# Expert gate and up weights read in 4 KB pieces, gathered rows turned by every fourth column

## The reference, cut to what matters

```python
he = jax.nn.silu(t @ w_exp_gate[e]) * (t @ w_exp_up[e])      # t: tokens x 1024, weights 1024 x 256
out = out + dense_w[:, e:e+1] * (he @ w_exp_down[e])         # 256 x 1024; dense_w: two experts of 16 per token
```

## Time and profile before

| what | value |
|---|---|
| median of 3 runs | 900.63 us |
| span of the profiled execution | 897.8 us |
| TensorE busy / weight loads busy | 97% / 82% of the span |
| VectorE, ScalarE, GpSimd busy | 51%, 44%, 20% |
| DMA q1 (SP) / q0 (GpSimd) | 38.1% / 10.6% of 16 engines' span |
| packets of q1 / q0 | 89,240 / 7,904 |
| mean granted TensorE clock | 0.990 |

### The profile page before, as it was taken

One profiled execution on the slowest core, in us unless ns is written; L12 is line 12 of the kernel. 1 busy time (PEld: TensorE's weight loads), 2 busy tenths in 40 slices (PEclk: granted clock), 3 DMA queues, 4 the chain that ended last, 5 costly groups with the idle time before them and its releaser, 6 DMA issues.

```text
span 897.8 us, 13732 instructions
## 1 busy us (share of the span) xinstructions
PE 867.1 (97%) x5236; PEld 735.5 (82%) x5236; DVE 461.4 (51%) x762; ACT 393.2 (44%) x549; POOL 178.5 (20%) x129
## 2 busy tenths in 40 slices
PE   8999999999999999999999999999988999899996
PEld 7988888898788888888888878888887878688863
DVE  5411355455429642324231246613588887777737
ACT  5432444454432543333434112214444767587643
POOL 0001010000100001100100000400003586867651
PEclk9999999999999999999999999999989999999998
DMA  9324132332121313231220211792859999988787
GB/s 296 115 68 88 48 77 58 67 69 56 38 70 41 94 48 64 74 87 47 32 77 18 93 47 52 242 398 100 296 201 329 339 379 381 382 315 291 255 288 301
DMA packets 97227, 141.95 MB, mean 158 GB/s; under 512 B 4566, under 2 KB 75430, under 8 KB 97094
## 3 DMA queue, kind: packets, MB, share of 16 engines
q1 hardware_dynamic: 89240, 114.52, 38.1%
q0 software_dynamic: 7904, 26.44, 10.6%
q10 hardware_dynamic: 32, 0.26, 0.3%
HBM read 116.31 MB, written 24.90 MB: 157 GB/s over the span
## 4 chain that ended last, share of the span: by engine, by line
PE 84%; DVE 6%; DMA 4%; issue 2%; ACT 2%; POOL 1%; ACTq 0%; SPq 0%; POOLq 0%; DVEq 0%
PE main L850 22%; PE main L851 21%; PE main L852 21%; PE work L934 3%; PE work L904 2%; DMA xg<-h_rows,column 2%; PE work L1134 2%; PE work L967 2%; PE work L951 2%; PE work L921 1%; PE work L1081 1%; DMA x_in<-in_x_prompt 1%; PE work L850 1%; PE work L852 1%; PE work L851 1%
## 5 line engine op out<-in xcount | busy, mean ns | idle before, releaser
L850 PE MATMUL main<-ht_hi,w_hi 128*128 128x512 f32 (+1 forms) x576 | 198.5, 345 | 0.0
L851 PE MATMUL main<-ht_lo,w_hi 128*128 128x512 f32 (+1 forms) x576 | 194.0, 337 | 0.0
L852 PE MATMUL main<-ht_hi,w_lo 128*128 128x512 f32 (+1 forms) x576 | 193.9, 337 | 0.0
L1586 DVE TENSOR_TENSOR w_lo<-raw,w_hi 128x2048 fp32r<-128x2048 f32 x29 | 66.4, 2291 | 234.7 <-ACT w_hi L1264 234.7
L850 PEld LDWEIGHTS main<-ht_hi,w_hi 128*128 128x128 f32 x576 | 109.2, 190 | 18.7 <-issue 5.2
L852 PEld LDWEIGHTS main<-ht_hi,w_lo 128*128 128x128 f32 x576 | 109.2, 190 | 11.9
L851 PEld LDWEIGHTS main<-ht_lo,w_hi 128*128 128x128 f32 x576 | 109.4, 190 | 11.0
L850 PE MATMUL main<-w_hi,ht_hi 128*128 128x256 f32 (+1 forms) x304 | 95.6, 315 | 0.1
L702 POOL DMA_DIRECT2D bias<-bias_vectors x16 | 12.4, 774 | 408.4 <-DVE nmx L1652 176.4
L852 PE MATMUL main<-w_hi,ht_lo 128*128 128x256 f32 (+1 forms) x304 | 92.8, 305 | 0.0
L851 PE MATMUL main<-w_lo,ht_hi 128*128 128x256 f32 (+1 forms) x304 | 92.8, 305 | 0.0
(11 more groups left out here) (308 smaller groups left out, 1576.2 us busy)
## 6 DMA issues: line engine op xcount, KB each, us to landing
e_raw<-in_w_exp_gate SPq DMA_DIRECT2D x16, 1024.0 KB, 8.6
e_raw<-in_w_exp_up SPq DMA_DIRECT2D x16, 1024.0 KB, 10.5
e_raw<-in_w_exp_down SPq DMA_DIRECT2D x16, 1024.0 KB, 8.8
raw<-in_w_in SPq DMA_DIRECT2D x30, 512.0 KB, 5.2
expert_rows<-y_sb SPq DMA_DIRECT2D x18, 512.0 KB, 8.6
raw<-in_w_in SPq DMA_DIRECT2D x8, 1024.0 KB, 5.3
expert_rows<-y_sb SPq DMA_DIRECT2D x1, 5632.0 KB, 22.9
raw<-in_w_out SPq DMA_DIRECT2D x4, 1024.0 KB, 5.4
```

What stands on the lines that cost most here:

```text
L850: pe.matmul(out, s_hi, m_hi, start=(first and i == 0), stop=False)
L851: pe.matmul(out, s_hi, m_lo, start=False, stop=False)
L852: last = pe.matmul(out, s_lo, m_hi, start=False, stop=(final and i == n - 1))
L1586: dve.tensor_tensor(w_lo[:, c % 2, :], raw[:, c % 2, :], w_hi[:, c % 2, :], ALU.subtract).then_inc(s_wlo, 1)
```

## The change

The rows of a gate or up weight are dealt out in another way: row 512h + 4p + b goes to partition p, half h, block b. A partition then reads two pieces of 4 rows, 4 KB each, where it read 8 pieces of 1 KB. In `e_raw` the 2048 numbers of a partition are still 8 blocks of 256, block k = 4h + b, so the splits and the products are unchanged. Block k now sums over rows 512h + 4p + b, so the transposes must bring column 512h + 4p + b of the gathered rows to partition p: the weight load of each transpose takes every fourth column of a half (a step of 16 bytes) instead of 128 neighbouring columns. The rows in `h2_rows` and the gathers stay as they are.

```diff
-        gate_v = w_exp_gate[0].rearrange("e (k p) n -> e p k n", p=P)
-        up_v = w_exp_up[0].rearrange("e (k p) n -> e p k n", p=P)
+        gate_v = w_exp_gate[0].rearrange("e (h p b) n -> e p h (b n)", h=2, p=P)
+        up_v = w_exp_up[0].rearrange("e (h p b) n -> e p h (b n)", h=2, p=P)
...
-                put = e8 if c < 2 else e2
+                put = e2
                 sp.dma_start(put(e_raw[j % 2][:, c, :]), expert_v[c][e]).then_inc(s_eraw[c][j % 2], 16)
...
-                    last = pe.transpose(xt_ps[:, P * k:P * k + P], xg[:, j % 2, P * k:P * k + P], ident[:, :])
+                    last = pe.transpose(xt_ps[:, P * k:P * k + P], xg[:, j % 2, 512 * (k // 4) + k % 4:512 * (k // 4 + 1):4], ident[:, :])
```

## The result

The changed kernel takes 898.58 us against 900.67 (medians of 22 runs each); the ratio is 0.9972, with an interval of 0.9961 to 0.9982. It is faster by 0.3%, 2 to 2.5 us, where 7.0 us were forecast. Its runs go from 895.5 to 902.8 us, those of the kernel before from 898.3 to 903.7, and a profile shows one of them. Its profiled execution spans 896.7 us (897.8 before). SP's queue has 64,664 packets, 24,576 fewer, as worked out.

The account below looks back on a forecast made before the run. TensorE, busy 97% of the span, was taken as the bound, idling in the experts' first part for weights short of DMA. Transposes 0 less 7.0 us for pieces took 900.6 to 893.6 us, range 892 to 909.

Parts of the forecast that it names:

- Pieces, the bandwidth: Gate and up loads: 4 KB pieces raise 372 GB/s to at most 418, a tile's DMA taking 10.0 us; gain 7.0 us.
- No load is late: Experts' first 9 tiles: a shortage of 0.7 us per tile uses up 6 us of a lead of 10.
- Next late is nothing: with the waits gone TensorE's own 9.31 us bounds each tile: Experts' tiles: once the waits for late weights go, no other limit follows and TensorE's work sets the tile time.
- ScalarE's 3.06 us: GpSimd's split of the down weight started 3.06 us late behind ScalarE, which had waited for that weight; hence the late gather.
- every named wait: TensorE's waits of 0.83, 1.21 and 2.97 us, plus 1.8 of slow clock: 6.8 us by name, all expected to go.
- Transposes at 0: Strided weight loads of 152 transposes: cost taken as 0, with an upper bound of 12.0 to 19.3 us.
- About 48 ns to spare: Transposes' weight loads of 144 ns: loads of 192 ns still fit the pace of 0.109 us, so that growth is hidden.
- Rival 2: Part of the strided loads shows, 20 to 45 ns per transpose: 896.6 to 900.4 us, middle 898.5; chance 0.12.
- Rival 1: Strided weight loads set the transposes' pace, a column costing as much as in L1108: slower, middle 908.4 us; chance 0.26.
- The Trainium skill's rule on 16-byte lines: Full speed wants at least two hits per 16-byte memory line; the strided transposes hit a new line per column, giving rival 1.
- The third rival: No bandwidth gained where it is short, or gathers land later among 4 KB pieces: no change, 900.6 us; chance 0.10.
- The sum: Whole kernel: transposes 0 less 7.0 us for the pieces, so the median goes from 900.6 to 893.6 us.

Follow-up runs that it names:

- e7_early: Changed kernel, but GpSimd copies the table's column for the next gather ahead of its split of the down weight; 895.0 us, ratio 0.9933.
- e6_nosplit: Changed kernel with GpSimd's split of the down weight in the loop cut to 64 of 2048 numbers; 895.5 us, ratio 0.9942.
- e7_again: Changed kernel with the table's column copied ahead of GpSimd's split, measured once more beside two other kernels on one chip; 895.96 us, ratio 0.9946.
- e5_eight: Kernel before with gate and up in one 8 KB piece per partition and transposes with a step of 8 numbers; 901.66 us, ratio 1.0017.
- e4_two: Kernel before with gate and up in 2 KB pieces and transposes with a step of 2 numbers; 898.77 us, ratio 0.9982.

## Why the prediction was wrong

- *Pieces, the bandwidth:* right in the main. All traffic at up to 418 GB/s was the upper bound; the rate went to 412 at full engines and 397 over 86 us once gathers no longer held the stage. ScalarE's waits for weights went from 9.9 us to none. The slow clock went in this trace; 4 KB pieces don't rule it out (mean clock down to 0.987 in single runs). "No load is late" would not have lasted: at 397 GB/s a tile's 4.19 million bytes take 10.6 us, not 10.0, and e7_early and e6_nosplit have waits for weights of 1.1 and 7.0 us again.
- *"Next late is nothing: with the waits gone TensorE's own 9.31 us bounds each tile":* this step failed. The earlier trace rows already had a gather issued 7.6 us after the split began, and an issue of 2.89 us. Between the two stands a copy that they leave out:

```profile
763.61 2.24 POOL L743 COPY column<-table_u 128x1 uint32 x1
```

I put all of it down to ScalarE's 3.06 us, the one part that a weight explained, and booked every named wait as a wait for weights. With weights in time, the chain of 17.5 us on GpSimd and in the queue still made gathers late: 4.3 us of waits. e7_early shows it: with the copy moved 0.3 us of them are left, the 9 tiles take 4.6 us less, and the runs 2.3 to 3.5 us less than the changed kernel's (by the ratios of e7_again and e7_early), about as much as the change gave.
- *Transposes at 0:* mis-sized. About 48 ns to spare was right: with loads 49 ns longer than 144 (e5_eight) the transposes are 0.112 us apart; in the changed kernel the loads grew by 64 ns, and 0.120 - 0.109 = 0.011 us per transpose came through, 19 x 0.07 = 1.3 us in all. Rival 2 names the mechanism, at half its lower price. That its middle, 898.5, is what was measured is luck: it takes the full gain of 7.0 less a price of 4.9, and neither came. Rival 1 was wrong: what a strided moving operand costs in L1108 did not hold for a weight load.
- *The Trainium skill's rule on 16-byte lines* (SBUF — State Buffer, section Door 1): the trace agrees that a step costs, 64 ns per load. It disagrees on where: a step of 8 bytes, two hits in each line, costs the same 64 (e4_two). The same section calls a step of 4 fp32 numbers free; for a weight load it is not.
- *The third rival* named gathers that are waited for as before. They were. But its reason, longer turns in the queues, is not borne out for 4 KB: among gathers whose issue VectorE held, and among the free ones, the times to the landing are those of the kernel before (table in the last section). Beside pieces of 8 KB the held ones take somewhat longer, 9.7 us after 9.2 on average and 10.8 at most, and the free ones don't.
- *The sum:* 7.0 forecast. In the traces the excess of the 9 tiles fell by 8.7 - 6.0 = 2.7 us, less 15 x 0.07 = 1.1 us of longer tiles over 15: 1.6. The stage begins 0.3 us later, so the spans differ by 1.1; the medians differ by 2.1.

## What to carry to other kernels

When a wait has a late input behind it, add up the whole chain from that input to the waiting instruction as if the input were in time, before the wait is booked as a gain; if the chain is longer than the slack, a second limit stands right behind the first. A small instruction that prepares the next transfer belongs in the idle time ahead of a long one on an in-order engine, not behind it: that alone was worth as much here as 24,576 packets, and both together gave about the sum. When an instruction takes twice its usual time in a row of the trace, look at what the other engines do at that moment. A strided weight load took some 50 to 70 ns longer here, and it is cheap only where the pace is set by something else.

## What the runs showed of the hardware

- A GpSimd instruction that starts while VectorE is inside a split of 128x2048 (L1769, 2.29 us) doesn't end before that does. In the rows above the copy starts at 714.59, 0.29 us after the first of two splits, and ends at 716.83, 0.24 us after that one's 2.29 us would be over. In both kernels the copies of the last tiles that meet VectorE's cast of 128x2048 (L1782, 1.22 us) take 1.18 or 1.19, and those that meet neither take 0.18 to 0.20. The gathers' issue behaves alike, 0.97 against 2.2 to 2.9 us. In e6_nosplit no copy or gather of the loop met one at its start, and they took 0.18 and 0.96 to 0.99; VectorE's copy of 128x1024 from `main` beside them held none. That it is a lock between the two engines is the Trainium skill's account (SBUF — State Buffer, section Who interferes with whom, which has it for a VectorE instruction with two SBUF inputs against a GpSimd one that reads SBUF); the times agree.
- A gather whose issue is held so lands later by about as much. Gathers issued from 700 to 790 us, mean time from the start of the issue to the landing (number of gathers):

| kernel, pieces | issue held, over 2 us | issue free, 0.97 us |
|---|---|---|
| before, 1 KB | 9.2 us (5) | 7.6 us (4) |
| changed, 4 KB | 9.3 us (6) | 7.4 us (3) |
| e5_eight, 8 KB | 9.7 us (5) | 7.6 us (3) |
| e7_early, 4 KB | 9.8 us (1) | 7.7 us (8) |
| e6_nosplit, 4 KB | none | 7.6 us (10) |

  Both gathers that TensorE waited for in the kernel before and all four in the changed one were held. How much of the early copy's gain is the earlier issue and how much the free one, no run separates.
- Full DMA engines move more with larger pieces: in the stretch from 720 to 735 us, with a share of 1.02 to 1.06, gate and up in pieces of 1 KB come with 380 GB/s, 2 KB with 403 (e4_two), 4 KB with 412, 8 KB with 422 (e5_eight).
- VectorE reads two operands with a step of 4 numbers at 1.15 us for 512 columns, 2.3 us for a row block of 1024, where neighbours take 1.28.
